# The closing projection of a two-block transformer kernel, taken token tile by token tile

## The reference, cut to what matters

```python
h = h + 0.5 * _rmsnorm(f, ffn2_post_g[i])
gate = jax.nn.sigmoid(_rmsnorm(h, ple_pre_g[i]) @ ple_w_gate[i])   # 256x1024 @ 1024x1024
e = p[i] @ ple_w_proj[i]                                            # 256x256 @ 256x1024
h = h + _rmsnorm(gate * e, ple_post_g[i])

def _rmsnorm(x, g):
    y = x * rsqrt(mean(x * x) + EPS)
    return y * g
```

## Time and profile before

| | us |
|---|---|
| three runs | 1150.89, 1150.79, 1149.94 |
| their median | 1150.79 |
| span of the profiled execution, first to last instruction | 1148.5 |
| TensorE busy in the span | 1137.1 (99%) |
| VectorE, ScalarE, GpSimd busy | 741.6, 589.4, 105.7 |

### The profile page before, as it was taken

How to read it: one execution, slowest core, us unless ns; L and a number is a source line. 1 busy time by engine, 2 the same in 40 slices (tenths; PEclk the granted TensorE clock), 3 DMA queues, 4 the chain that set the end, 5 groups by cost and what they waited for, 6 DMA issues and landing times.

```text
span 1148.5 us, 16462 instructions
## 1 busy us (share of the span) xinstructions
PE 1137.1 (99%) x6408; PEld 993.3 (86%) x6408; DVE 741.6 (65%) x931; ACT 589.4 (51%) x788; POOL 105.7 (9%) x162
## 2 busy tenths in 40 slices
PE   9999999999999999999999999999999999999997
PEld 8998888888889999988888898899888888889885
DVE  6866686657777888754664554665866566545465
ACT  5674654446565766543554443564554364444353
POOL 6410211000011000000000000200500010000020
PEclk9999999999999999999999999999999999999999
DMA  9643753455634765564665656465457467555641
GB/s 252 206 156 97 223 185 110 164 201 184 217 132 138 251 207 176 187 215 147 209 214 182 186 174 209 154 213 181 145 187 239 146 229 234 192 168 175 213 137 72
DMA packets 122894, 209.81 MB, mean 183 GB/s; under 512 B 10965, under 2 KB 58186, under 8 KB 122827
## 3 DMA queue, kind: packets, MB, share of 16 engines
q1 hardware_dynamic: 119225, 198.64, 54.2%
q10 hardware_dynamic: 3506, 10.23, 2.4%
q0 software_dynamic: 96, 0.01, 0.1%
HBM read 207.67 MB, written 1.18 MB: 182 GB/s over the span
## 4 chain that ended last, share of the span: by engine, by line
PE 94%; DVE 3%; DMA 1%; ACT 1%; issue 0%; POOL 0%; POOLq 0%; DVEq 0%; SPq 0%; ACTq 0%
PE ACCP L867 28%; PE ACCP L869 28%; PE ACCP L868 28%; PE SMP L1068 3%; DVE CONVF L2301 1%; PE SMP L1061 1%; DVE LO L2176 1%; DMA RAW<-in_w_in_dram 1%; DMA X<-in_x_dram 0%; PE SMP L1221 0%; PE SMP L1237 0%; PE SMP L1021 0%; PE SMP L1016 0%; PE SMP L1015 0%; PE SMP L1406 0%
## 5 line engine op out<-in xcount | busy, mean ns | idle before, releaser
L2176 DVE TENSOR_TENSOR LO<-RAW,HI 128x1024 fp32r<-128x1024 f32 x365 | 438.1, 1237 | 231.3 <-ACT HI L1607 225.0
L1607 ACT ACTIVATE HI<-RAW 128x1024 fp32r<-128x1024 f32 x366 | 370.1, 1054 | 269.6 <-PE ACCP L869 222.6
L867 PE MATMUL ACCP<-HI,XH 128*128 128x512 f32 x704 | 277.4, 394 | 0.0
L869 PE MATMUL ACCP<-HI,XL 128*128 128x512 f32 x704 | 274.4, 390 | 0.0
L868 PE MATMUL ACCP<-LO,XH 128*128 128x512 f32 x704 | 274.0, 389 | 0.0
L867 PE MATMUL ACCP<-XH,HI 128*128 128x256 f32 x640 | 182.0, 284 | 0.7 <-DVE CONVF L2301 0.7
L869 PE MATMUL ACCP<-XH,LO 128*128 128x256 f32 x640 | 181.1, 283 | 0.0
L868 PE MATMUL ACCP<-XL,HI 128*128 128x256 f32 x640 | 181.1, 283 | 0.0
L869 PEld LDWEIGHTS ACCP<-HI,XL 128*128 128x128 f32 x704 | 132.1, 188 | 27.8
L868 PEld LDWEIGHTS ACCP<-LO,XH 128*128 128x128 f32 x704 | 132.3, 188 | 26.2
L867 PEld LDWEIGHTS ACCP<-HI,XH 128*128 128x128 f32 x704 | 132.3, 188 | 26.2
(11 more groups left out here) (416 smaller groups left out, 1144.5 us busy)
## 6 DMA issues: line engine op xcount, KB each, us to landing
RAW<-in_w_in_dram SPq DMA_DIRECT2D x104, 512.0 KB, 4.5
RAW<-in_w_up_dram SPq DMA_DIRECT2D x44, 512.0 KB, 4.4
RAW<-in_ffn_w_gate_dram SPq DMA_DIRECT2D x44, 512.0 KB, 4.6
RAW<-in_ffn_w_up_dram SPq DMA_DIRECT2D x44, 512.0 KB, 4.5
RAW<-in_ffn_w_down_dram SPq DMA_DIRECT2D x44, 512.0 KB, 4.4
RAW<-in_w_down_dram SPq DMA_DIRECT2D x22, 512.0 KB, 4.2
RAW<-in_w_out_dram SPq DMA_DIRECT2D x8, 512.0 KB, 4.4
RAW<-in_w_mkv_dram SPq DMA_DIRECT2D x8, 512.0 KB, 4.3
```

Of the source, the lines that this page charges most:

```text
L867: pe.matmul(dst, lhs[0], rhs[0], start=start, stop=False)
L869: return pe.matmul(dst, lhs[1], rhs[0], start=False, stop=stop)
L1607: act.activation(HI[:, n % RING, half_of(half)], RAW[:, n % RAWS, half, :], ACT.Copy).then_inc(hi_ready, 1)
L2176: dve.tensor_tensor(LO[:, s, c], RAW[:, n % RAWS, half, :], HI[:, s, c].bitcast(f32), ALU.subtract).then_inc(lo_ready[s], 1)
```

## The change

1. `T_OPEN["ple_g"]` goes from 3 to 4: all four blocks are multiplied with tile 0 first, and `norm_turn` for tile 1 moves to the place before block 3. TensorE signals tile 0's first 512 columns after block 1 and the second after block 3.
2. For tile 1, blocks 0 and 1 are taken as before. Columns 512 to 1023 come as two chunks of 256 columns (`last_chunk`), each over all eight 128-row steps of the contraction, 24 matmuls of 256 columns each. The first goes to bank 3, the second to bank 0, whose sums of tile 0 ACT has taken by then (`last_gate`).
3. ACT takes five sigmoids (three of 512 columns, two of 256), and sums no squares. DVE does for each of the five pieces: product, sum of squares started from the sum of the piece before (so that the last one is the row's whole sum), gain. POOL is left with one power per tile.
4. The roots and sums of the very first norm are written at another place in the code; the instructions are the same.

```diff
-T_OPEN = {"mix_v": 4, "ple_g": 3, "ffn1": 4, "ffn2": 4}
+T_OPEN = {"mix_v": 4, "ple_g": 4, "ffn1": 4, "ffn2": 4}
...
+        def last_sums(q):
+            return (acc("ple_g", Turn(1), 1), acc("ple_g", Turn(0), 0))[q][:, 0:256]
...
-            for t in range(NT):
-                pool.wait_ge(first_sq, t + 1)
-                pool.wait_ge(last_sq, t + 1)
-                mean_square = POST[:, 2 * t:2 * t + 1]
-                link(pool.tensor_tensor(mean_square, mean_square, POST[:, 2 * t + 1:2 * t + 2], ALU.add))
-                pool.tensor_tensor(ROOT[f"last.{t}"], mean_square, MINUS_HALF[:, 0:1], ALU.pow).then_inc(root_ready, 1)
+            for t, pieces in ((0, 2), (1, 5)):
+                pool.wait_ge(gated_sums, pieces)
+                pool.tensor_tensor(ROOT[f"last.{t}"], POST[:, pieces - 1:pieces], MINUS_HALF[:, 0:1], ALU.pow).then_inc(root_ready, 1)
...
+            def last_chunk():
+                pe.wait_ge(last_gate, 1)
+                for q in range(2):
+                    dst = last_sums(q)
+                    for kk in range(KT):
+                        s = lo_is_ready(pe, "ple_g", Turn(2 + kk // 4))
+                        c = slice(kk % 4 * 512 + q * 256, kk % 4 * 512 + q * 256 + 256)
+                        last = three(dst, (XH[:, kk, tok(1)], XL[:, kk, tok(1)]), (HI[:, s, c], LO[:, s, c]), kk == 0, kk == KT - 1)
+                    last.then_inc(block_done, 1)
...
+                        if phase == "ple_g" and m == 1 and j == 2:
+                            last_chunk()
+                            return
                         last = t_part(phase, j, m, XH, XL, norm_ready(r, m), by_half=m == 0)
                         if m == 1:
                             last.then_inc(block_done, 1)
+                        elif phase == "ple_g" and j % 2 == 1:
+                            last.then_inc(tile_done, 1)
...
-            for m in range(NT):
-                t_part("ple_g", 3, m, XH, XL).then_inc(block_done if m == 1 else tile_done, 1)
...
-                    if chunk == 1:
-                        act.wait_ge(last_product, m + 1)
-                        act.activation(EP[:, m, 512:DM], PG[:, m, 512:DM], ACT.Square, scale=DM ** -0.5,
-                                       accum_out=POST[:, 2 * m + 1:2 * m + 2]).then_inc(last_sq, 1)
+            act.wait_ge(tile_done, len(TILED) + 1)
+            gate(0, 0)
+            act.wait_ge(tile_done, len(TILED) + 2)
+            gate(0, 1)
+            act.wait_ge(block_done, FIRST["ple_g"] + 2)
+            gate(1, 0)
+            for q in range(2):
+                act.wait_ge(block_done, FIRST["ple_g"] + 2 + q + 1)
+                act.activation(PG[:, 1, 512 + q * 256:768 + q * 256], last_sums(q), ACT.Sigmoid).then_inc(last_gate, 1)
...
+            def gated_piece(n, t, part, before):
+                small_is_taken(dve, f"ple.{t}{'ab'[part.start // 512]}")
+                dve.wait_ge(last_gate, n + 1)
+                link(dve.tensor_tensor(PG[:, t, part], PG[:, t, part], EP[:, t, part], ALU.mult))
+                dve.tensor_tensor_reduce(out=EP[:, t, part], in0=PG[:, t, part], in1=PG[:, t, part], scale=1.0 / DM, scalar=before,
+                                         op0=ALU.mult, op1=ALU.add, accum_out=POST[:, n:n + 1]).then_inc(gated_sums, 1)
+                dve.wait_ge(gated_sums, n + 1)
+                dve.tensor_tensor(PG[:, t, part], PG[:, t, part], POST_GAIN[:, part], ALU.mult).then_inc(gain_done, 1)
...
+            gated_piece(0, 0, slice(0, 512), EPS)
+            gated_piece(1, 0, slice(512, DM), POST[:, 0:1])
+            add_gated(0, 2)
+            gated_piece(2, 1, slice(0, 512), EPS)
+            gated_piece(3, 1, slice(512, 768), POST[:, 2:3])
+            gated_piece(4, 1, slice(768, DM), POST[:, 3:4])
+            add_gated(1, 5)
```

More of the change, by code:

```diff
@@ L358, in build @@
         MINUS_HALF = stat(16)
-        MEAN, LSS, POST = stat(2), stat(2), stat(4)
+        MEAN, LSS, POST = stat(2), stat(2), stat(5)
         FFN_SS, MIX_SS = stat(2), stat(2)
@@ L388, in build @@
         half_sumsq = sem("half_sumsq")
-        first_sq, last_product = sems("first_sq last_product")
+        last_gate, gated_sums = sems("last_gate gated_sums")
         gain_zeroed, gain_row_loaded, gain_spread = sems("gain_zeroed gain_row_loaded gain_spread")
@@ L411, in build @@
         y2_ready, y2_hi, y2_lo = sems("y2_ready y2_hi y2_lo")
-        p_hi, last_sq, out_ready = sems("p_hi last_sq out_ready")
+        p_hi, gain_done, out_ready = sems("p_hi gain_done out_ready")
         class Turn:
@@ L484, in tile_is_done @@
                 eng.wait_ge(tile_done, list(TILED).index(phase) + 1)
[L485 to L488, removed]
             else:
@@ L726, in norm_root @@
                 total = SS[r][:, t:t + 1]
[L727 to L732, removed]
                 if r == "norm_ffn":
@@ L772, in _ @@
             link(pool.memset(MINUS_HALF, -0.5))
-            norm_roots("norm_mix")
+            for t in range(NT):
+                pool.wait_ge(mix_sq, t + 1)
+                pool.wait_ge(sumsq, t + 1)
+                total = SS["norm_mix"][:, t:t + 1]
+                link(pool.tensor_tensor(total, total, MIX_SS[:, t:t + 1], ALU.add))
+                pool.tensor_tensor(ROOT[f"norm_mix.{t}"], total, MINUS_HALF[:, 0:1], ALU.pow).then_inc(root_ready, 1)
             for half in range(2):
@@ L2146, in _, with gate @@
             split_ahead("ple_e", Turn(0))
[L2147 to L2154, removed]
-                    if chunk == 1:
-                        act.wait_ge(last_product, m + 1)
-                        act.activation(EP[:, m, 512:DM], PG[:, m, 512:DM], ACT.Square, scale=DM ** -0.5,
-                                       accum_out=POST[:, 2 * m + 1:2 * m + 2]).then_inc(last_sq, 1)
+            def gate(m, chunk):
+                act.activation(PG[:, m, chunk * 512:(chunk + 1) * 512], acc("ple_g", Turn(chunk), m), ACT.Sigmoid).then_inc(last_gate, 1)
+            act.wait_ge(tile_done, len(TILED) + 1)
[7 more added lines that the diff above has]
+                act.activation(PG[:, 1, 512 + q * 256:768 + q * 256], last_sums(q), ACT.Sigmoid).then_inc(last_gate, 1)
         @block.vector
@@ L2247, in y_split, with mix_sum @@
                     dve.tensor_tensor(lo, src, hi.bitcast(f32), ALU.subtract).then_inc(bank_of(name), 1)
+            def mix_sum(t):
+                dve.wait_ge(x_loaded[t], 16)
+                dve.tensor_tensor_reduce(out=XS[:, t, 512:DM], in0=X[:, t, 512:DM], in1=X[:, t, 512:DM], scale=1.0 / DM, scalar=EPS,
+                                         op0=ALU.mult, op1=ALU.add, accum_out=MIX_SS[:, t:t + 1]).then_inc(mix_sq, 1)
             def mix_scale(t, b):
@@ L2265, in _ @@
             for t in range(NT):
-                dve.wait_ge(x_loaded[t], 16)
-                dve.tensor_tensor_reduce(out=XS[:, t, 512:DM], in0=X[:, t, 512:DM], in1=X[:, t, 512:DM], scale=1.0 / DM, scalar=EPS,
-                                         op0=ALU.mult, op1=ALU.add, accum_out=MIX_SS[:, t:t + 1]).then_inc(mix_sq, 1)
+                mix_sum(t)
             mix_scale(0, 0)
@@ L2862, in _, with add_gated @@
             split_ahead("ple_e", Turn(0))
[L2865 to L2885, removed]
+            def gated_piece(n, t, part, before):
[6 more added lines that the diff above has]
+                dve.tensor_tensor(PG[:, t, part], PG[:, t, part], POST_GAIN[:, part], ALU.mult).then_inc(gain_done, 1)
+            def add_gated(t, pieces):
                 root = root_is_ready(f"last.{t}")
+                dve.wait_ge(gain_done, pieces)
                 for half in range(2):
@@ L2890, in add_gated @@
                                              op0=ALU.mult, op1=ALU.add).then_inc(out_ready, 1)
-            for t in range(NT):
-                gated_half(t, 0)
             dve.wait_ge(post_gain_loaded, 16 * 4)
[L2895 to L2902, removed]
+            gated_piece(0, 0, slice(0, 512), EPS)
[5 more added lines that the diff above has]
+            add_gated(1, 5)
 def kernel(**inputs):
```

## The result

| | median of runs, us | lowest to highest | span of the profiled execution |
|---|---|---|---|
| before | 1150.55 (8 runs) | 1149.94 to 1150.93 | 1148.5 |
| changed | 1153.95 (8 runs) | 1152.19 to 1155.31 | 1152.2 |

What follows compares the result with a forecast made beforehand. TensorE, busy 1137.1 of 1148.5 us, was taken as the bound, so only its waits and the work behind its last matmul count. +3.3 + 0.3 - 1.55 = +2.1 us, from 1150.79 to 1152.9; range 1151.8 to 1155.2.

Steps and rivals of the forecast that it cites:

- The stall: TensorE, right behind tile 1's transposes, waits for block 3's first low half from DVE: 3.3 us, bounds 3.2 to 3.4.
- The second low half: Block 3's other low half on DVE follows 1.2 us later; six matmuls taking 1.36 cover it, so no second stall.
- The pace: The 48 new 256-column matmuls on TensorE, at 0.120 us a step, take 5.76 us against 5.47: +0.3 us.
- The end: Work behind the last matmul, from last sigmoid to last scaling: 2.31 us in place of 3.86, -1.55 us.
- What costs nothing: DVE's gain (0.42) runs during POOL's power (0.65); tile 0's old sums never on the path; DVE's longer order and loads have time.
- stall of 3.3 us, full clock: Forecast case: TensorE stalls behind tile 1's transposes, granted clock stays 1.00; 1152.9 us, with scatter 1151.8 to 1153.8; 76%.
- the slower clock: Rival: clock falls before or during block 3's matmuls, costing 1.6 to 3.2 us more, 1154.5 to 1156.1; 17%.
- the prediction's own sign against the forecast: A stall under 2 us, or TensorE steps of 0.45 us behind it, would make the forecast wrong.
- The rival's price: Low grant for 3.3 us behind the stall: some 7 matmuls at 0.456 in place of 0.228, 1.6 us; twice as long, 3.2.
- Slower by over 0.2%: Chance that the changed kernel measures above 1153.1 us: 0.27 from the forecast case plus 0.17 from the slower clock, 0.44.

Runs made afterwards that it cites:

- the last experiment: The changed kernel with block 3's split moved ahead of tile 1's XH and XL split, plus tile 1's last 512 columns as one piece: 1149.55 us.

## Why the prediction was right or wrong

**The stall**: right in place, cause and size. 3.3 us were forecast from the train of work behind the transposes, 3.2 found; it went when the split of block 3 was moved, and when the order was put back. The second low half made no second stall, as said.

**The pace**: right. 0.120 us a step, +0.3 us.

**The end**: right in its sum, 2.34 us where 2.31 stood, by some luck. Within the sum small misses cancelled: the power took 0.79 where 0.65 stood and the sum of squares 0.49 (1146.93 to 1147.42) where 0.44 stood, while the sigmoid with its hand-over took 0.48 where 0.53 stood, and the two hand-overs around the power 0.12 where 0.24 stood. The 0.92 taken from the earlier trace rows as the power's upper bound was not the price of "the later of two chained instructions": it was a power beside a gain. (The upper bound of the sum adds up to 2.64, not 2.67; nothing hangs on it.)

**What costs nothing**: right for TensorE and the loads, and VectorE was never late. Two things were missed. The gain on VectorE was to run free of charge beside the power; it did run beside it, but the power took 0.79 us in place of the 0.55 that it takes with VectorE idle, so that 0.24 us of it were on the path. No run here takes the gain away from the power; the wider gain of the last experiment, which lengthened it by 0.26, is the nearest. And the prediction named the old sums of tile 0 as "never on the path". They were not in the old order, but under the new one they would have been, for 0.9 us; the change's two halves belong together. The sum was not touched by this, since the changed kernel has both.

**The choice among the cases**: this is the step that failed. The text took "stall of 3.3 us, full clock" as the likeliest, at 76%, and the slower clock as a rival at 17%. The profiled execution, and at least half of the eight runs by their mean clock, show the rival, and the prediction's own sign against the forecast (steps of 0.45 us behind the stall) came up at 0.43. The forecast of the full-clock case, 1152.9, is what the kernel takes when TensorE is kept busy in the gap (1152.88). The measured 1153.95 lies between the two cases, since it is the median of runs with and without a fall. It is outside the 1151.8 to 1153.8 of the forecast case and inside the range only because that took in the lower half of the rival.

The rival's price came out by luck. It was 1.6 us, from the 3.3 us for which the rows of before show the low grant; 1.7 were measured, and 1154.5 forecast for it. But those 3.3 us end where the span ends. The trace of before goes on behind the span: the grant is 0.50 in the window 1148.5 to 1150.5 and 1.00 from 1150.6 on, so it was low for 5.4 us in all. And a step at the low grant took 0.43 us, not the 0.456 that was reckoned.

What misled was to compare 3.3 us with the 4 us after which the clock was still 1.00 behind the last matmul, as if that time were fixed: the row was a single draw. The nine traces, read in windows of 0.1 us, show how far it varies:

| where TensorE fell idle | us from then until the grant fell | us at 0.50 |
|---|---|---|
| changed kernel, behind the last matmul | 1.9 | 6.4 |
| before with the moved split, behind the last matmul | 2.7 | 7.1 |
| last half row in one piece, behind the last matmul | 2.8 | 6.5 |
| before, behind the last matmul | 4.4 | 5.4 |
| split of block 3 first, behind the last matmul | 4.4 | 3.9 |
| new end alone, behind the last matmul | 4.5 | 3.8 |
| six needless matmuls, behind the last matmul | 4.6 | 3.7 |
| reordering alone, behind the last matmul | 4.8 | 5.9 |
| twelve needless matmuls, behind the last matmul | 5.0 | 3.3 |
| reordering alone, in the gap | 2.7 | 3.4 |
| changed kernel, in the gap | 3.6 | 3.4 |

Behind the last matmul it took from 1.9 to 5.0 us, and three of the nine are shorter than the 2.9 us for which TensorE sat idle in the gap. In the reordering alone the grant fell 0.3 us before the matmuls came back; in the changed kernel 0.7 us after the first of them; in some runs, by their mean clock, not at all. "Slower by over 0.2%" with 0.44 was too low for the same reason.

What stays open: what decides, in one run, when the clock falls and for how long. No run here varies that by itself.

## What to carry to other kernels

When a block is consumed earlier, follow its preparation back through each engine's program order: here both engines had about 5 us of idle time ahead of the step that was late, and the step only stood behind one that waited. A wait of some 3 us on TensorE can cost more than itself, since the matmuls behind it ran at half clock in at least nine of the thirteen runs here that have such a wait and leave TensorE idle in it; put the preparation first or, failing that, keep TensorE busy. Do not take a delay for fixed because the one trace at hand shows it once. Test the halves of a change apart and together, since here the order alone cost 5.75 us, the end alone gained 1.2, and the two together cost 3.4, not 4.5.

## What the runs showed of the hardware that was not expected

- A gap in which TensorE sat idle for 2.9 us (3.2 us lost) let the clock fall to 0.50, by the mean clocks in at least four runs of eight in the changed kernel and in all five of the reordering alone; with an idle time of 1.6 us no run of eleven shows a fall in its mean clock, with 0.2 us none of ten.
- Behind the last matmul the grant fell after 1.9 to 5.0 us in the nine traces, and stayed at 0.50 for 3.3 to 7.1 us.
- With twelve needless matmuls in the gap the kernel took 1152.88 us and with six 1152.25, against 1153.95 without. These are other sets of runs; over their own before they stand 2.5, 2.0 and 3.4 us.
- The sum of squares that starts from another piece's sum took 0.75 us for 512 columns, the one that starts from a constant 0.69 (VectorE in the changed kernel).
- The same power of one column on GpSimd took 0.55 us with VectorE idle at its start, and 0.79, 0.88 or 1.05 beside a gain on VectorE: in all 16 such cases at the end of these kernels it ended 0.40 to 0.42 us after VectorE's instruction, which read two operands in SBUF.
